# When TensorE asks for the second of two weight units

## The reference

```
x = x + rms_norm(merged @ w_out, norm_post)          # "wo" in the kernel
h = h + merged @ w_o[i]                              # "wp"
return o @ w_xo                                      # "xo", added to h
```

## Time and profile before

| | |
|---|---|
| median of 3 runs | 1136.04 us (1135.01 to 1136.5) |
| profiled execution, own time | 1137.02 us |
| its span, first to last instruction | 1135.2 us |
| TensorE busy | 1033.0 us (91%) |
| GpSimd busy | 549.5 us (48%) |
| mean granted TensorE clock | 0.964 of full |

### The profile page before, as it was taken

One profiled execution on the slowest core, in us unless ns is written; L12 is line 12 of the kernel. 1 busy time (PEld: TensorE's weight loads), 2 busy tenths in 40 slices (PEclk: granted clock), 3 DMA queues, 4 the chain that ended last, 5 costly groups with the idle time before them and its releaser, 6 DMA issues.

```text
span 1135.2 us, 19570 instructions
## 1 busy us (share of the span) xinstructions
PE 1033.0 (91%) x7820; PEld 862.2 (76%) x7820; DVE 613.6 (54%) x1345; ACT 424.7 (37%) x632; POOL 549.5 (48%) x411
## 2 busy tenths in 40 slices
PE   5998999988967889999999899999997899998894
PEld 4887888888957779999977789988986555665552
DVE  7957446368545875553239986631124744444444
ACT  5554333332225546554544344444343011211112
POOL 4665734357746976664776458978743000000000
PEclk9999898999987989999999999999999999999997
DMA  7554512333332544343432325446465969999992
GB/s 289 201 196 165 208 50 75 110 133 130 128 131 97 186 164 149 116 144 113 149 117 106 112 75 188 183 148 213 158 251 200 403 267 371 419 419 420 420 420 101
DMA packets 32051, 224.96 MB, mean 198 GB/s; under 512 B 3680, under 2 KB 3808, under 8 KB 5216
## 3 DMA queue, kind: packets, MB, share of 16 engines
q1 hardware_dynamic: 31104, 220.62, 51.4%
q10 hardware_dynamic: 864, 3.15, 0.8%
HBM read 273.04 MB, written 1.05 MB: 241 GB/s over the span
## 4 chain that ended last, share of the span: by engine, by line
POOL 39%; issue 28%; PE 23%; DMA 4%; DVE 4%; ACT 1%; POOLq 0%; ACTq 0%; DVEq 0%
POOL wlo L541 39%; PE ps L2434 6%; DMA ring<-in_experts 4%; PE ps L2375 3%; PE ps L2446 3%; PE ps L1831 2%; PE ps L1832 2%; PE ps L1833 2%; PE ps L2462 2%; PE ps L2420 0%; DVE stat L943 0%; DVE xlo L975 0%; DMA x<-in_x 0%; DVE xcf L1088 0%; DVE stat L946 0%
## 5 line engine op out<-in xcount | busy, mean ns | idle before, releaser
L541 POOL TENSOR_TENSOR wlo<-raw,whi 128x512 fp32r<-128x512 f32 x406 | 549.1, 1387 | 314.6 <-ACT whi L567 314.4
L1883 PE MATMUL ps<-xhi,whi 128*128 128x256 f32 x960 | 282.2, 294 | 14.3 <-DVE xlo L1211 4.1
L1884 PE MATMUL ps<-xhi,wlo 128*128 128x256 f32 x960 | 276.4, 288 | 0.0
L1885 PE MATMUL ps<-xlo,whi 128*128 128x256 f32 x960 | 276.0, 287 | 0.0
L567 ACT ACTIVATE whi<-raw 128x2048 fp32r<-128x2048 f32 x112 | 213.9, 1915 | 140.2 <-PE ps L1885 65.7
L1883 PEld LDWEIGHTS ps<-xhi,whi 128*128 128x128 f32 x960 | 189.1, 197 | 18.5 <-issue 11.8
L1884 PEld LDWEIGHTS ps<-xhi,wlo 128*128 128x128 f32 x960 | 189.4, 197 | 1.0 <-issue 0.7
L1885 PEld LDWEIGHTS ps<-xlo,whi 128*128 128x128 f32 x960 | 189.1, 197 | 0.0
L1831 PE MATMUL ps<-whi,xhi 128*128 128x512 f32 (+3 forms) x298 | 117.3, 394 | 6.6 <-DVE xlo L975 4.3
L1832 PE MATMUL ps<-wlo,xhi 128*128 128x512 f32 (+3 forms) x298 | 114.5, 384 | 0.0
L1833 PE MATMUL ps<-whi,xlo 128*128 128x512 f32 (+3 forms) x298 | 114.5, 384 | 0.0
(11 more groups left out here) (465 smaller groups left out, 1481.7 us busy)
## 6 DMA issues: line engine op xcount, KB each, us to landing
ring<-in_experts SPq DMA_DIRECT2D x144, 1024.0 KB
raw<-in_weights SPq DMA_DIRECT2D x112, 1024.0 KB, 4.8
x<-in_x SPq DMA_DIRECT2D x2, 512.0 KB, 4.7
memt<-in_mem ACTq DMA_DIRECT2D x1, 1024.0 KB, 7.6
decay<-in_decay ACTq DMA_DIRECT2D x1, 512.0 KB, 3.7
npost<-in_norm_post ACTq DMA_DIRECT2D x1, 512.0 KB, 5.5
nfin<-in_norm_final ACTq DMA_DIRECT2D x1, 512.0 KB, 7.7
out<-xn SPq DMA_DIRECT2D x2, 256.0 KB, 2.5
```

The source lines that it names most:

```text
L541: ins = pool.tensor_tensor(wlo[:, j, c], raw[:, j, c], whi[:, j, c].bitcast(f32), ALU.subtract)
L1883: mm(o_, wh[:, k, cc], hi[:, k0 + r0 + k, :], start=first, stop=False, skip_group_check=True)
L1884: mm(o_, wl[:, k, cc], hi[:, k0 + r0 + k, :], start=False, stop=False, skip_group_check=True)
L1885: ins = mm(o_, wh[:, k, cc], lo[:, k0 + r0 + k, :], start=False, stop=last, skip_group_check=True)
```

## The change

`pair_ends` called `parts` for both units before its first product, so TensorE waited for both. Now each unit's wait stands directly before that name's products of token tile 0: TensorE waits for the first unit, does its 12 products of tile 0, then waits for the second unit and does its 12, and then tile 1 of both as before.

```diff
             def pair_ends(a, b, hi, lo, k0=0):
-                w = [parts(UNIT[name][1], 4, 512) for name in (a, b)]
-                for t in range(TT):
-                    for name, (wh, wl) in zip((a, b), w):
+                w = {}
+                for t in range(TT):
+                    for name in (a, b):
+                        if t == 0:
+                            w[name] = parts(UNIT[name][1], 4, 512)
+                        wh, wl = w[name]
                         tok = slice(t * P, t * P + P)
                         for k in range(4):
                             ins = mm3(...)
```

## The result

The changed kernel takes 1125.4 us (median of 4 runs, 1124.13 to 1126.86); the kernel before, run beside it, 1135.53 (1134.02 to 1136.5). The ratio is 0.9925 (95% interval 0.99 to 0.9949), 8.5 us by the ratio and 10.1 by the medians. The profiled execution took 1126.86 us, its span 1125.1. The forecast was 1126.8, with a range of 1124.3 to 1130.9.

The account below looks back on a forecast made before the run. Neither TensorE (91% busy) nor GpSimd's subtraction was taken to bound the whole; they hand the path to each other. Work 6.8 plus clock 2.4 gave 9.2 us off 1136.04: forecast 1126.8 us, range 1124.3 to 1130.9.

Parts of the forecast that it names:

- Which unit was late: At pairs wo, wp and xo the first unit was ready when TensorE came; it stood for the second.
- The work: Filling the waits ahead of the pairs with the first name's 12 products gains 2.81, 1.63 and 2.36 us, 6.8 in all.
- The clock: Low-clock stretches at pairs wo and wp go away: 1.6 us counted at wo, 0.8 at wp, none at xo.
- Rival (a): Work is filled but the clock is not regained: 1129.2 us, or 1130.9 with one more low stretch; chance 0.18.
- xo's stop of 2.18 us as proof: xo's clock stayed 1.00 after 2.18 us, so wo's remaining 0.6 us stop does no harm; its 1.6 us counted whole.
- Carried to the end: The gains of all three pairs reach the kernel's end, 9.2 us let through whole.
- it moves by what that moves: The norm behind wo begins with the second name's tile 0 and moves as much as that, about 4.4 us.
- (b): Behind xo, expert-weight transfers set the last stretch and xo's part is lost: 6.8 us gained, 1129.2 us; chance 0.06.
- (c): GpSimd takes all back, as TensorE comes earlier to units not there: 1136 us, no change; chance 0.05.
- (d): TensorE's 0.6 us pause inside wo's pair keeps the clock low through what follows: slower, 1143 us; chance 0.03.
- the 2.6 of the forecast: TensorE's waits on GpSimd's subtraction for 512-column products fall from 8.9 to about 2.6 us.

Follow-up runs that it names:

- discarded products: Kernel before, with TensorE filling the stop ahead of each pair with products thrown away (12 at wo, 6 at wp, 9 at xo): 1131.39 us, ratio 0.9971.
- wo's alone: Kernel before, with only the pair wo asking late for its second unit: 1133.14 us, ratio 0.9976; run once more, 1131.23 us.
- xo's alone: Kernel before, with only the pair xo asking late for its second unit: 1134.53 us, ratio 0.9976.
- small pieces: Changed kernel with GpSimd's subtraction in pieces of 256 columns instead of 512, twice as many: 1142.04 us, ratio 1.0083 against the kernel before.
- changed, again: The changed kernel, unchanged, run once more for a second profile: 1125.9 us, ratio 0.9919 against the kernel before.

## Why the prediction was right

**Which unit was late.** Right at all three pairs: with its wait alone behind it, the first name's products started 0.24 us (wo) and 0.22 us (xo) behind the last product ahead, and at wp 0.41 us behind the start of the last four transposes (734.73 and 735.14), as one of them follows the other.

**The work.** Forecast 2.81, 1.63 and 2.36 us. Taking the clock's part of the discarded products off the distances leaves 3.41 - 1.51 = 1.90 at wo, with the 0.9 that VectorE's step cost it 2.8; 3.22 - 1.59 = 1.63 at wp; 2.46 at xo. The sizes hold.

**The clock.** Forecast 1.6 at wo and half of 1.6 at wp. Measured 1.5 and 1.6: at wp I took half because the stop of 0.97 us and the transposes stay, and that was too careful by 0.8. Rival (a), filled work without the clock, did not come: the clock was 1.00 in each of the 22 changed pairs that were profiled. At xo the forecast said that the clock is full in any case, and that failed: the two profiles with 19.13 and 19.18 us show a low stretch on it after the same stop. The sum put nothing there because the one profile that it rested on had none. With 1.6 us in two of five, the change gains some 0.65 us more in the mean, 9.7 in place of 9.1 (an estimate from these five). The step that took xo's stop of 2.18 us as proof that a shorter one does no harm was weak for the same reason, though what it forecast came.

**Carried to the end.** At wo the step "it moves by what that moves" failed in its size. The pair's last product started 6.64 us early (327.13 against 333.77) and the last one ahead of it 2.33, which is 4.3 as forecast (4.4), but the norm behind it moved by only 3.4: starting earlier, its first VectorE step fell beside GpSimd's last subtraction and waited 0.9 us for it. I had written that GpSimd holds nothing back there, and looked only at who waits for its result, not at who runs beside it. The 0.9 lost here and the 0.8 won at wp nearly cancel, so 9.2 was forecast and 9.1 came: that the sum is so close is luck. Behind that all was carried: wo's alone to the end, xo's alone past the router and to the transfers. Rivals (b) and (c) fell. Against (c) the way from the first transpose u to the last one ahead of wp's pair is 399.81 us before and 399.86 changed, so that GpSimd took nothing back on it.

**(d), the slower one,** fell: the clock was 1.00 through wo's pair although TensorE paused 0.45 us in its middle (2.38 us in "small pieces"). So the Trainium skill's case of a clock that swings on short pauses (same page, A second HAM failure mode: psum-queue depth-cycling) was not this one.

**Against the median.** The forecast of 9.2 us compares with 10.1 by the medians of the first runs, 9.5 by those of the later ones, and 8.5 to 9.2 by the two ratios. TensorE's wait for the subtraction fell to 1.3 us, further than the 2.6 of the forecast, but to 4.0 in "changed, again": outside the pairs it varies.

## What to carry to other kernels

Place a wait directly ahead of the first instruction that needs it: where a group begins with work on two buffers, ask for the second behind the first one's share, as long as the order in which results are finished stays. When a stop of TensorE is filled, count the clock too, as it was a third of this gain (3.1 of 9.1 us); products thrown away got that third alone. Don't take the clock of a stretch from one profile: look at the same stretch in several. When a chain is moved earlier, look at what it then runs beside, not only at what it waits for.

## What the runs showed of the hardware

Some VectorE steps with both inputs in SBUF stood until GpSimd's unbroken run of subtractions was over: 10.77 us for an addition of 0.9, 15.8 for one on 32 columns, 27.65 and 12.99 in small pieces; each ended within 0.6 us of the end of a run. It comes by chance in one execution and not in the next: 2 of the 12 profiles with pieces of 512 columns had one, and each set TensorE back by some 9 us, which is large beside the change. Whether it makes the spread of the kernel before, 1128.34 to 1144.17 us, is not shown, as neither of its two profiles has one; the low-clock stretches that fall elsewhere are a rival. The Trainium skill (SBUF — State Buffer, SBUF: two separate sides) calls the ports that both engines share an exclusive lock, held for one instruction, with the other engine blocked. The block agrees with the trace; held for one instruction it would not be enough, as VectorE was kept out while 8 to 39 GpSimd instructions in a row began. That the ports are the cause here is the page's reading and was not tested apart. Why some steps get in between two pieces (L1531 with 0.87 us in the kernel before) and others don't was not settled; a pause put into GpSimd's stream on purpose was not tried.
